# Two attention branches between dense products on one core: plain fp32 products grouped into eight bursts in two pairs of heads, score tiles at other distances, and the long branch's first turn taken from the first query tiles

## The chip, the cores and the metric

The kernel runs on one core of a Trainium2 chip. The metric is the device time of one execution in microseconds (us), lower is better. The program has 48,305 profiled instructions; nearly all of them are the work of one loop over eight blocks of 512 tokens.

## The reference

One encoder layer over 4096 tokens of width 1024, everything in fp32:

```python
h = rms_norm(x, norm_g)
proj = h @ w_in                      # 1024 -> 5376 columns, split into
(qa, ka, va, za, qb, kb, vb, zb, ga, gb)
# branch A: 8 query heads on 2 key heads of 64, own chunk of 64 and the one before,
#           partial rotary on qa and ka, an attention sink per head
# branch B: 8 heads of 64, own chunk and 8 chunks before, learned relative bias
ya = swa_sink_attention(rope(qa), rope(ka), va, sinks) * silu(za)
yb = chunked_relpos_attention(qb, kb, vb, rel_bias) * silu(zb)
merged = sigmoid(ga + bias0) * (ya @ w_br_a) + sigmoid(gb + bias1) * (yb @ w_br_b)
out = rms_norm(x + merged @ w_out, final_g)
```

## The kernel before, in words

**Blocks and pairs.** A block is 512 tokens, four tiles of 128. Its heads are worked off in eight pairs in the order 0, 4, 1, 5, 2, 6, 3, 7: pairs 0 to 3 are of branch A (the short branch, a query tile sees 256 keys), pairs 4 to 7 of branch B (the long branch, 640 keys). So short and long pairs alternate.

**Two kinds of product on TensorE.** The dense projections take three matmuls of 128x512 per slice of weights (high times high, low times high, high times low), on operands of type fp32r, lines L909 to L911. A "quarter" is six of them; a tile of weights has four quarters. Attention uses plain fp32 operands, in three steps:

- S0 to S3 ("scores"): the scores of query tile 0 to 3 of the *next* pair, L944 (short) and L953 (long), into the banks sc. VectorE then masks, adds the bias and takes the row maxima (L1242 to L1268); ScalarE takes the exponentials (E0 to E3, L1146) and so frees the score bank.
- T0, T1, ... ("turn_p"): a turn transposes up to four 128x128 pieces of the probabilities into the one bank ps_pt (L973). ScalarE (L1153) or VectorE (L1329) then copies the bank to one of four probs_t; a list per branch, A_OUT and B_OUT, says which (0 is ScalarE). PE waits before each turn until the turn before it is copied out.
- V0, V1, ... ("values"): probabilities times values into ps_o (L1004). Which keys a burst takes stands in A_BURSTS and B_BURSTS, which pieces a turn takes in A_TURNS and B_TURNS, as (half of the pair, key tile), where key tiles below 0 belong to the block before. The first V of a pair waits until VectorE has read the pair before out of ps_o (`whole`, L1366).

**The order.** All engines walk one list, PLAN, each taking from it its own steps; each engine works strictly in that order. Within a pair the order is written by hand in the strings A_BEATS and B_BEATS, where F is one quarter of dense products, T, V, S and E are the steps above, G and H the gating of the pair before, D the denominators. Each string has twelve F, so three tiles of weights. After the fourth F, and once a tile is at its second or third quarter, the step "norm" (N below) is put in: four transposes on PE into a bank of acc (L1013), read by VectorE (L1360).

**Rotary.** When a tile q or k of the short branch is complete, ScalarE copies it (pre, L1098) and rounds it (pre_hi, L1101), VectorE makes pre_lo (L1304) and pre*cos (L1308). PE multiplies by a permutation (L1024, L1025, called R below) into a bank of acc, and VectorE reads that (L1316), which frees the bank. For pairs 1, 2 and 3 the step R is put in front of a quarter of the following tile of weights, `fill[at_ + 3]` being that tile's fourth; for pair 0 and the keys it is in the list `lead`.

Of the kernel before, what the change touches and what calls it, by code (L numbers as in the profile page):

```python
# [24 lines left out]
D = 1024  # L25
# [22 lines left out]


A_TURNS = [[(0, 0), (1, 0)], [(0, 1), (1, 1)], [(0, 2), (1, 2)], [(0, 3), (1, 3), (0, -1), (1, -1)]]  # L50
B_TURNS = [[(0, -1)], [(1, -1)], [(0, 0)], [(1, 0)], [(0, -2)], [(1, -2)], [(0, 1)], [(1, 1)],
           [(0, -3), (1, -3)], [(0, 2), (1, 2)], [(0, -4), (1, -4), (0, 3), (1, 3)]]

A_BURSTS = [[0], [1], [2], [3, -1]]
B_BURSTS = [[-1], [0], [-2], [1], [-3], [2], [-4, 3]]

A_OUT = (0, 1, 1, 0)
B_OUT = (0, 1, 0, 1, 0, 0, 1, 0, 0, 1, 0)
RING = 4


def turns_of(s):
    return A_TURNS if s < PAIRS else B_TURNS


def bursts_of(s):
    return A_BURSTS if s < PAIRS else B_BURSTS

# [8 lines left out]
def segments(s, u, first):  # L77


    out, col = [], 0  # L80
    for hh, j in turns_of(s)[u]:
        if first and j < 0:
            continue
        t0, n = queries_of(s, j)
        out.append((hh, j, t0, n, col))
        col += n * P
    assert col <= BLK
    return out
# [27 lines left out]
O_BANKED = 2  # L116


A_BEATS = "T0 F G T1 V0 F H D T2 V1 S0 F E0 T3 V2 F S1 V3 F E1 F F S2 F E2 F F S3 F E3 F"
B_BEATS = "F T0 F G T1 F H D T2 V0 F T3 F T4 V1 S0 F T5 E0 F T6 V2 S1 F T7 E1 F T8 V3 S2 F T9 E2 V4 S3 T10 F E3 V5 F V6"  # L120
BEATS_QUARTERS = 12
NORM_AFTER = 4
EARLY = 1
# [6 lines left out]
def block_plan():  # L130
# [11 lines left out]
    def tile(name, n):  # L142
        i = TILES.index((name, n))
        return [[("mm", i, c)] for c in range(QUARTERS - 1)] + [[("mm", i, QUARTERS - 1), ("job", name, n)]]

    def tiles(first, last):

        return [g for t in TILES[TILES.index(first):TILES.index(last) + 1] for g in tile(*t)]

    q, v, k4 = tile("q", 0), tile("v", 0), tile("k", 4)  # L150
    lead = [[("mm", n, c)] for n in range(O_TILES) for c in range(QUARTERS)]
    lead[0] = [("claim_v",), *lead[0]]
    lead[-1] = [*lead[-1], ("v_out",)]
    lead += [*tile("k", 0), q[0], [*q[1], ("rope_in_k", 0)], q[2], [("rope_k", 0), *q[3]],
             v[0], [*v[1], ("rope_in", 0)], v[2], [("rope", 0), *v[3]], [("turn_v", 0), *k4[0]], *k4[1:], *tile("q", 4)]
    for t in range(TT):
        at_ = QUARTERS * O_TILES + 14 + t
        lead[at_] = [("scores", 0, t), *lead[at_], ("exps", 0, t)]
# [7 lines left out]
    fill = tiles(("z", 0), ("gb", AHEAD - 1))  # L166
    first_fill = TILES.index(("z", 0))
    for i in range(first_fill, TILES.index(("gb", AHEAD - 1)) + 1):
        name, s = TILES[i]
        at_ = QUARTERS * (i - first_fill + 1)  # L170
        if name == "q" and s < PAIRS:
            fill[at_] = [*fill[at_], ("rope_in", s)]
            fill[at_ + 3] = [("rope", s), *fill[at_ + 3]]
    fill += [[("mm", TILES.index(("br", 0)), 0)], [("mm", TILES.index(("br", 0)), 1), ("job", "ya", 0)]]

    for n, s in enumerate(ORDER):
        nxt = ORDER[n + 1] if n + 1 < SETS else None
        quarters = 0
        for beat in (A_BEATS if s < PAIRS else B_BEATS).split():
            kind, no = beat[0], int(beat[1:] or 0)  # L180
# [50 lines left out]
    for e in range(KT):  # L231
# [4 lines left out]
        for c in range(QUARTERS):  # L236
            plan.append(("mm", i, c))
            at_ = QUARTERS * e + c
# [21 lines left out]


PLAN = block_plan()


# [57 lines left out]
def turn_table(first):  # L322

    no, on = {}, [0, 0]
    for step in PLAN:
        if step[0] == "turn_p" and segments(step[1], step[2], first):
            engine = (A_OUT if step[1] < PAIRS else B_OUT)[step[2]]
            on[engine] += 1
# [1151 lines left out]
```

## Time and profile before

| what | value |
|---|---|
| median of 3 runs | 3419.65 us (3418.62 to 3423.51) |
| the profiled execution's own time | 3421.02 us |
| its span in the trace | 3419.2 us |
| TensorE matmuls busy | 3342.8 us, 98% |
| VectorE, ScalarE, GpSimd busy | 1482.7, 1422.4, 1309.1 us |
| granted TensorE clock | 0.999 |

The span begins with the first profiled instruction; the time of an execution lies 1.8 us above it. A busy TensorE is not one at its peak, because the ends of matmuls are modelled: what a stretch costs on PE is read from one start to the next.

### The profile page before, as it was taken

To read this page: it belongs to the slowest core of one execution; us is meant where nothing else is said; L and a number is where in the kernel's file an instruction comes from. 1 tells how busy PE (TensorE), PEld (TensorE's weight loads), DVE (VectorE), ACT (ScalarE), POOL (GpSimd) and SP (SyncE) were. 2 spreads that over 40 slices of the span, in tenths; PEclk is the share of its full clock that TensorE was granted. 3 is DMA by queue.
4 is the path that set the end of the run, shared out by engine and by line. 5 is a ranking of instruction groups with operands and counts; after the bars stand their busy time and mean duration, and the time that the engine had idled before them with its cause. 6 is when DMAs were issued, how large, how long until landed. Compare 5 with 4: busy or idle time off the path is not lost.

```text
span 3419.2 us, 48305 instructions
## 1 busy us (share of the span) xinstructions
PE 3342.8 (98%) x16328; PEld 2496.7 (73%) x16328; DVE 1482.7 (43%) x3097; ACT 1422.4 (42%) x2969; POOL 1309.1 (38%) x1087
## 2 busy tenths in 40 slices
PE   7999999999999999999999999999999999999998
PEld 6667876678766787667876678766787667876676
DVE  4662355513555135551355513555135551355512
ACT  4443444434444344443444434444344443444432
POOL 3334542344423454234542345423454234542244
PEclk9999999999999999999999999999999999999999
DMA  4212431124311242112421225211242112521123
GB/s 156 62 62 88 171 99 50 62 87 167 99 51 62 86 169 97 55 61 83 173 93 55 61 83 173 93 56 62 81 172 94 56 61 83 173 94 55 56 82 116
DMA packets 97782, 319.53 MB, mean 93 GB/s; under 512 B 9984, under 2 KB 26624, under 8 KB 95360
## 3 DMA queue, kind: packets, MB, share of 16 engines
q1 hardware_dynamic: 97536, 316.34, 28.5%
q8 instruction: 144, 2.36, 0.3%
q14 instruction: 102, 0.84, 0.1%
HBM read 299.52 MB, written 16.78 MB: 93 GB/s over the span
## 4 chain that ended last, share of the span: by engine, by line
PE 84%; issue 7%; DVE 5%; POOL 2%; ACT 1%; DMA 0%; DVEq 0%; POOLq 0%; SPq 0%; ACTq 0%
PE acc L909 16%; PE acc L911 14%; PE acc L910 14%; PE ps_o L1004 6%; PE ps_pt L973 5%; PE sc L953 3%; PE sc L909 3%; PE sc L911 3%; PE sc L910 3%; POOL w_lo L755 2%; PE sc L944 2%; PE sc L853 2%; PE sc L852 2%; PE sc L851 2%; PE sc L876 1%
## 5 line engine op out<-in xcount | busy, mean ns | idle before, releaser
L755 POOL TENSOR_TENSOR w_lo<-w_raw,w_hi 128x512 fp32r<-128x512 f32 x928 | 1210.3, 1310 | 2048.1 <-ACT w_hi L1058 2046.9
L909 PE MATMUL acc<-h_hi,w_hi 128*128 128x512 f32 x2432 | 1012.1, 416 | 15.5 <-DVE q L1316 15.5
L911 PE MATMUL acc<-h_hi,w_lo 128*128 128x512 f32 x2432 | 953.1, 392 | 0.0
L910 PE MATMUL acc<-h_lo,w_hi 128*128 128x512 f32 x2432 | 950.4, 391 | 0.0
L1058 ACT ACTIVATE w_hi<-w_raw 128x512 fp32r<-128x512 f32 x928 | 574.4, 625 | 393.1 <-DMA w_raw<-w 118.0
L909 PEld LDWEIGHTS acc<-h_hi,w_hi 128*128 128x128 f32 x2432 | 456.4, 188 | 228.5 <-issue 146.5
L911 PEld LDWEIGHTS acc<-h_hi,w_lo 128*128 128x128 f32 x2432 | 456.4, 188 | 101.7
L910 PEld LDWEIGHTS acc<-h_lo,w_hi 128*128 128x128 f32 x2432 | 458.1, 188 | 75.4
L1146 ACT ACTIVATE probs_b<-sc,negm 128x640 f32<-128x640 f32 x256 | 202.9, 794 | 390.3 <-DVE negm L1263 390.2
L1153 ACT ACTIVATE probs_t<-ps_pt 128x512 f32<-128x512 f32 (+1 forms) x272 | 150.7, 554 | 264.7 <-PE ps_pt L973 264.7
L1288 DVE SCALAR_TENSOR_TENSOR part<-th,sc 128x512 f32<-128x512 f32 x64 | 43.9, 686 | 467.9 <-PE sc L911 467.7
L1329 DVE COPY probs_t<-ps_pt 128x512 f32<-128x512 f32 (+1 forms) x188 | 125.3, 667 | 250.7 <-PE ps_pt L973 250.2
L1263 DVE TENSOR_REDUCE negm<-sc 128x1 f32<-128x640 f32 x256 | 211.0, 824 | 8.9
L909 PE MATMUL sc<-y_hi,w_hi 128*128 128x512 f32 x512 | 201.6, 394 | 6.0 <-DVE y_lo L1376 6.0
L911 PE MATMUL sc<-y_hi,w_lo 128*128 128x512 f32 x512 | 199.4, 390 | 0.0
L910 PE MATMUL sc<-y_lo,w_hi 128*128 128x512 f32 x512 | 199.3, 389 | 0.0
L973 PE MATMUL ps_pt<-ident,probs_b 128*128 128x128 f32 x1200 | 187.0, 274 | 6.2 <-DVE probs_t L1329 6.2
L973 PEld LDWEIGHTS ps_pt<-ident,probs_b 128*128 128x128 f32 x1200 | 147.6, 141 | 52.9 <-DVE probs_t L1329 8.6
L1255 DVE TENSOR_TENSOR sc<-sc,bias 128x256 f32<-128x256 f32 (+2 forms) x512 | 184.5, 360 | 2.9
L1116 ACT ACTIVATE th<-acc,gb_half 128x512 f32<-128x512 f32 x128 | 88.1, 688 | 218.9 <-PE acc L911 218.9
L1004 PE MATMUL ps_o<-probs_t,v_b 128*64 128x512 f32 (+1 forms) x960 | 175.9, 455 | 1.0 <-DVE probs_t L1329 0.3
L953 PE MATMUL sc<-k_b,q 64*128 64x320 f32 (+3 forms) x992 | 164.3, 448 | 3.6 <-ACT probs_b L1146 3.6
(140 smaller groups left out, 3916.4 us busy)
## 6 DMA issues: line engine op xcount, KB each, us to landing
w_raw<-w SPq DMA_DIRECT2D x464, 512.0 KB, 3.5
rows<-x SPq DMA_DIRECT2D x36, 512.0 KB, 7.4
xt<-x_t SPq DMA_DIRECT2D x16, 1024.0 KB, 10.0
out<-rows SPq DMA_DIRECT2D x32, 512.0 KB, 2.8
x_in<-x SPq DMA_DIRECT2D x28, 512.0 KB, 5.5
cs<-rope_tab SPq DMA_DIRECT2D x8, 512.0 KB, 4.3
bias<-near SPq DMA_DIRECT2D x1, 1024.0 KB, 13.5
g_out<-final_g SPq DMA_DIRECT2D x1, 512.0 KB, 11.6
```

What stands on the lines that cost most here:

```text
L755: pool.tensor_tensor(w_lo[n % 2][:, c], w_raw[n % 2][:, c], w_hi[n % 2][:, c].bitcast(FP32), ALU.subtract).then_inc(w_split, 1)
L909: pe.matmul(dst[:, :], hi, src_hi[:, k, :], start=begin, stop=False)
L910: pe.matmul(dst[:, :], hi, src_lo[:, k, :], start=False, stop=False)
L911: mm = pe.matmul(dst[:, :], lo, src_hi[:, k, :], start=False, stop=end)
L953: mm = pe.matmul(sc[hh][:, c, lo:B_HALF], q[n % 2][rows_, t * P:(t + 1) * P], k_b[rows_, s - PAIRS, t * P + c * B_HALF + lo:t * P + (c + 1 ...
L973: mm = pe.transpose(ps_pt[:, col + (t - t0) * P:col + (t - t0 + 1) * P], weights_of(s, hh, t)[:, r * P:(r + 1) * P], ident[:, :])
L1004: mm = pe.matmul(ps_o[HD * hh:HD * hh + HD, t0 * P:(t0 + n) * P], val, ring(first, turn)[:, col:col + n * P], start=j == every[0], stop=j ...
L1058: act.activation(w_hi[n % 2][:, c], w_raw[n % 2][:, c], ACT.Copy).then_inc(w_hi_done, 1)
L1146: act.activation(p_, score_tile(s, hh, t), ACT.Exp, bias=negm[:, POS[s] % 2, c:c + 1], accum_out=sums[:, POS[s] % 2, c:c + 1]).then_inc(pr ...
L1153: act.activation(ring(first, turn)[:, 0:n], ps_pt[:, 0:n], ACT.Copy).then_inc(pt_out[0], 1)
L1255: dve.tensor_tensor(dst, dst, tab, ALU.add).then_inc(scores_shaped, 1)
L1263: dve.tensor_reduce(nm, score_tile(s, hh, t), AX.XY, ALU.max, negate=True).then_inc(neg_ready, 1)
```

## The change

Five tables and two places in `block_plan` are edited. No instruction is added or removed; the order changes, and with it who copies out which turn.

```diff
-B_TURNS = [[(0, -1)], [(1, -1)], [(0, 0)], [(1, 0)], [(0, -2)], [(1, -2)], [(0, 1)], [(1, 1)],
-           [(0, -3), (1, -3)], [(0, 2), (1, 2)], [(0, -4), (1, -4), (0, 3), (1, 3)]]
+B_TURNS = [[(0, -3), (1, -3)], [(0, -1)], [(1, -1)], [(0, 0)], [(1, 0)], [(0, -2)], [(1, -2)], [(0, 1)],
+           [(1, 1)], [(0, 2), (1, 2)], [(0, -4), (1, -4), (0, 3), (1, 3)]]
-B_BURSTS = [[-1], [0], [-2], [1], [-3], [2], [-4, 3]]
+B_BURSTS = [[-1], [-3], [0], [-2], [1], [2], [-4, 3]]
-B_OUT = (0, 1, 0, 1, 0, 0, 1, 0, 0, 1, 0)
+B_OUT = (0, 1, 0, 1, 0, 1, 0, 0, 1, 1, 0)
-A_BEATS = "T0 F G T1 V0 F H D T2 V1 S0 F E0 T3 V2 F S1 V3 F E1 F F S2 F E2 F F S3 F E3 F"
-B_BEATS = "F T0 F G T1 F H D T2 V0 F T3 F T4 V1 S0 F T5 E0 F T6 V2 S1 F T7 E1 F T8 V3 S2 F T9 E2 V4 S3 T10 F E3 V5 F V6"
+A_BEATS = "T0 F G T1 F H D T2 V0 V1 S0 T3 F E0 F F S1 V2 V3 F E1 F F S2 F E2 F F S3 F E3"
+B_BEATS = "T0 F G T1 F H D T2 F T3 V0 V1 S0 F T4 E0 F T5 F T6 F V2 V3 S1 T7 F E1 T8 F T9 F V4 V5 S2 T10 F E2 F V6 S3 E3"
-    lead += [*tile("k", 0), q[0], [*q[1], ("rope_in_k", 0)], q[2], [("rope_k", 0), *q[3]],
-             v[0], [*v[1], ("rope_in", 0)], v[2], [("rope", 0), *v[3]], [("turn_v", 0), *k4[0]], *k4[1:], *tile("q", 4)]
+    lead += [*tile("k", 0), [*q[0], ("rope_in_k", 0)], q[1], [("rope_k", 0), *q[2]], q[3],
+             [*v[0], ("rope_in", 0)], v[1], [("rope", 0), *v[2]], v[3], [("turn_v", 0), *k4[0]], *k4[1:], *tile("q", 4)]
-            fill[at_ + 3] = [("rope", s), *fill[at_ + 3]]
+            fill[at_ + 2] = [("rope", s), *fill[at_ + 2]]
```

**Bursts.** Between two F of the beats there can stand a group with S or V in it. Before, a short pair has six such groups (T1 V0; T2 V1 S0; T3 V2; S1 V3; S2; S3) and a long pair seven (T2 V0; T4 V1 S0; T6 V2 S1; T8 V3 S2; T9 V4 S3 T10; V5; V6). Now each has four: T2 V0 V1 S0 T3, S1 V2 V3, S2 and S3 in a short pair, T3 V0 V1 S0, V2 V3 S1 T7, V4 V5 S2 T10 and V6 S3 in a long one. The last long pair of a block issues no S.

**From a long pair to a short one, ScalarE's row.** These are ScalarE's instructions in the loop over blocks, at the end of pair 5 and the start of pair 2, before the change. probs_a are the exponentials E3 of the short pair's last query tile, pre and pre_hi belong to the rotary of q3, and the last L1153 copies out the short pair's first turn T0.

```order
L1142 REGISTER_ALU
L1146 ACTIVATE probs_a_85,sums<-sc,negm 128x256
L581 ISA
L598 REGISTER_ALU
L1058 ACTIVATE w_hi_53<-w_raw_51 128x512
L542 REGISTER_ALU
L1097 REGISTER_ALU
L1098 ACTIVATE pre<-acc 128x512
L547 REGISTER_ALU
L1101 ACTIVATE pre_hi<-pre 128x512
L1152 REGISTER_ALU
L1153 ACTIVATE probs_t_76<-ps_pt 128x512
```

And now:

```order
L1098 ACTIVATE pre<-acc 128x512
L547 REGISTER_ALU
L1101 ACTIVATE pre_hi<-pre 128x512
L1142 REGISTER_ALU
L1146 ACTIVATE probs_a_84,sums<-sc,negm 128x256
L1142 REGISTER_ALU
L1146 ACTIVATE probs_a_85,sums<-sc,negm 128x256
L1152 REGISTER_ALU
L1153 ACTIVATE probs_t_76<-ps_pt 128x512
L1164 REGISTER_ALU
L1167 ACTIVATE y_hi<-whole 128x512
L1058 ACTIVATE w_hi_53<-w_raw_51 128x512
```

E3 stood ahead of a split of weights and the rotary copies; now it is the last thing in front of the copy of T0.

**From a short pair to a long one, PE's row.** This is PE between the last scores of pair 1 and the turn T1 or T0, before the change: the last of the three quarters behind S3, and then the long pair's first turn, of all four query tiles.

```order
L909 MATMUL acc<-h_hi,w_hi_53 128x512
L910 MATMUL acc<-h_lo,w_hi_53 128x512
L911 MATMUL acc<-h_hi,w_lo_55 128x512
L909 MATMUL acc<-h_hi,w_hi_53 128x512
L910 MATMUL acc<-h_lo,w_hi_53 128x512
L911 MATMUL acc<-h_hi,w_lo_55 128x512
L966 REGISTER_ALU
L973 MATMUL ps_pt<-ident,probs_b_72 128x128 x4
```

Now the first turn (two pieces of each half; its second row is the first one here) comes one quarter behind S3, and the turn of all four query tiles after one more:

```order
L973 MATMUL ps_pt<-ident,probs_b_73 128x128 x2
L801 REGISTER_ALU
L899 REGISTER_ALU
L909 MATMUL acc<-h_hi,w_hi_53 128x512
L910 MATMUL acc<-h_lo,w_hi_53 128x512
L911 MATMUL acc<-h_hi,w_lo_55 128x512
L909 MATMUL acc<-h_hi,w_hi_53 128x512
L910 MATMUL acc<-h_lo,w_hi_53 128x512
L911 MATMUL acc<-h_hi,w_lo_55 128x512
L966 REGISTER_ALU
L629 REGISTER_ALU
L973 MATMUL ps_pt<-ident,probs_b_72 128x128 x4
```

The turn of four query tiles moved one quarter nearer to the scores, and it stands behind another turn now.

**The rotary product of pair 2, PE's row,** within pair 1. Before, it follows the scores S2, and a quarter lies between the N step (L1013, in the row just above these) and it:

```order
L909 MATMUL acc<-h_hi,w_hi_53 128x512
L910 MATMUL acc<-h_lo,w_hi_53 128x512
L911 MATMUL acc<-h_hi,w_lo_55 128x512
L909 MATMUL acc<-h_hi,w_hi_53 128x512
L910 MATMUL acc<-h_lo,w_hi_53 128x512
L911 MATMUL acc<-h_hi,w_lo_55 128x512
L923 REGISTER_ALU
L953 MATMUL sc<-k_b,q_62 128x320 x4
L801 REGISTER_ALU
L1023 REGISTER_ALU
L1024 MATMUL acc<-pre_hi,perm_r 128x512
L1025 MATMUL acc<-pre_lo,perm_r 128x512
```

Now:

```order
L909 MATMUL acc<-h_hi,w_hi_53 128x512
L910 MATMUL acc<-h_lo,w_hi_53 128x512
L911 MATMUL acc<-h_hi,w_lo_55 128x512
L909 MATMUL acc<-h_hi,w_hi_53 128x512
L910 MATMUL acc<-h_lo,w_hi_53 128x512
L911 MATMUL acc<-h_hi,w_lo_55 128x512
L801 REGISTER_ALU
L1013 MATMUL acc<-ident,part 128x128 x4
L801 REGISTER_ALU
L1023 REGISTER_ALU
L1024 MATMUL acc<-pre_hi,perm_r 128x512
L1025 MATMUL acc<-pre_lo,perm_r 128x512
```

R follows N at once. Both write the same bank of acc, and by the kernel's rule of claims R waits until VectorE has read N out of it; that read (L1360) stands on VectorE behind the masks and maxima of S1, which PE issued one quarter earlier. VectorE's pre_lo and pre*cos (L1304, L1308), which stood behind those of S1, stand ahead of them now.

## Rows read from the trace of the kernel before

**Rows 1.** The page, part 1: busy time, share of the span, instructions.

```profile
PE 3342.8 (98%) x16328; PEld 2496.7 (73%) x16328; DVE 1482.7 (43%) x3097; ACT 1422.4 (42%) x2969; POOL 1309.1 (38%) x1087
```

**Rows 2.** The waits of PE: who for whom, us in total, times, longest.

```profile
PE acc L909 <- DVE q L1316: 15.5, 15, 1.7
...
PE ps_pt L973 <- DVE probs_t L1329: 6.2, 18, 1.1
```

**Rows 3.** Timeline of PE, a V alone between products: start us, us, instruction.

```profile
1015.75 0.40 PE L911 MATMUL acc<-h_hi,w_lo 128*128 128x512 f32 x1
1016.08 0.65 PE L1004 MATMUL ps_o<-probs_t,v_b 128*64 128x256 f32 x4
1016.66 0.50 PE L909 MATMUL acc<-h_hi,w_hi 128*128 128x512 f32 x1
1017.00 0.40 PE L910 MATMUL acc<-h_lo,w_hi 128*128 128x512 f32 x1
```

**Rows 4.** Timeline of PE, a turn alone between products.

```profile
1048.69 0.39 PE L911 MATMUL acc<-h_hi,w_lo 128*128 128x512 f32 x1
1048.92 0.60 PE L973 MATMUL ps_pt<-ident,probs_b 128*128 128x128 f32 x4
1049.27 0.48 PE L909 MATMUL acc<-h_hi,w_hi 128*128 128x512 f32 x1
1049.59 0.40 PE L910 MATMUL acc<-h_lo,w_hi 128*128 128x512 f32 x1
...
1050.75 0.60 PE L973 MATMUL ps_pt<-ident,probs_b 128*128 128x128 f32 x4
```

**Rows 5.** Timeline of all engines from S3 of short pair 2 on.

```profile
1013.58 0.59 PE L944 MATMUL sc<-k_a,q 64*128 64x192 f32 x4
...
1014.10 0.66 PE L973 MATMUL ps_pt<-ident,probs_b 128*128 128x128 f32 x4
1014.27 0.11 DVE L1242 MEMSET sc<- 128x64 f32 x1 [0.48 <-PE sc L944]
...
1014.52 0.47 PE L909 MATMUL acc<-h_hi,w_hi 128*128 128x512 f32 x1
...
1016.25 0.47 ACT L1146 ACTIVATE probs_a<-sc,negm 128x256 f32<-128x256 f32 x1 [0.40 <-DVE negm L1268]
...
1016.72 0.62 ACT L1058 ACTIVATE w_hi<-w_raw 128x512 fp32r<-128x512 f32 x1
```

**Rows 6.** Timeline of all engines from S3 of long pair 6 on.

```profile
1043.42 1.35 PE L953 MATMUL sc<-k_b,q 64*128 64x320 f32 x8
...
1044.70 0.50 PE L909 MATMUL acc<-h_hi,w_hi 128*128 128x512 f32 x1
...
1047.70 0.68 DVE L1366 TENSOR_TENSOR whole<-ps_o,gate 128x512 f32<-128x512 f32 x1
...
1047.82 0.80 ACT L1146 ACTIVATE probs_b<-sc,negm 128x640 f32<-128x640 f32 x1 [0.61 <-DVE negm L1263]
...
1048.61 0.62 ACT L1058 ACTIVATE w_hi<-w_raw 128x512 fp32r<-128x512 f32 x1
...
1049.61 0.59 ACT L1153 ACTIVATE probs_t<-ps_pt 128x512 f32<-128x512 f32 x1
```

**Rows 7.** Timeline of all engines, PE waiting for a turn's copy.

```profile
1057.05 0.68 DVE L1329 COPY probs_t<-ps_pt 128x512 f32<-128x512 f32 x1
...
1057.79 0.55 PE L973 MATMUL ps_pt<-ident,probs_b 128*128 128x128 f32 x3 [0.18 <-DVE probs_t L1329]
```

**Rows 8.** Timeline of all engines around pair 1's rotary product.

```profile
979.54 0.39 PE L911 MATMUL acc<-h_hi,w_lo 128*128 128x512 f32 x1
...
980.82 0.68 DVE L1316 TENSOR_TENSOR q<-acc,cs 128x512 f32<-128x512 f32 x1
...
981.63 0.49 PE L909 MATMUL acc<-h_hi,w_hi 128*128 128x512 f32 x1 [1.70 <-DVE q L1316]
```

**Rows 9.** Timeline of all engines from a rotary copy on.

```profile
1018.45 0.60 ACT L1098 ACTIVATE pre<-acc 128x512 f32<-128x512 f32 x1 [1.11 <-PE acc L911]
...
1019.74 0.69 DVE L1304 TENSOR_TENSOR pre_lo<-pre,pre_hi 128x512 fp32r<-128x512 f32 x1 [3.52 <-ACT pre_hi L1101]
...
1021.14 0.68 DVE L1366 TENSOR_TENSOR whole<-ps_o,gate 128x512 f32<-128x512 f32 x1
...
1022.08 0.65 PE L1004 MATMUL ps_o<-probs_t,v_a 128*64 128x256 f32 x4 [0.75 <-DVE whole L1366]
```

## The prediction, as it was put on record

> **What bounds the kernel now.** I read the page first: matmuls are busy for 98% of the span while the other three engines stand below 45% [rows 1]. So PE sets the end, and only two things can move the time: what PE's own row costs from start to start, and how long PE stands still. The table of waits shows that it hardly stands still: its two largest groups inside the loop are 15.5 us for VectorE's read of a rotary product and 6.2 us for turns that are not copied out yet [rows 2]. Then I read the timeline for the price of changing between the two kinds of product. The reader is to look at starts, since ends are modelled. Products start 0.23 us apart, and a turn comes 0.23 us behind a product too (1048.69 to 1048.92) [rows 4]. But a V comes 0.33 us behind one (1015.75 to 1016.08), and behind the V the second product starts 0.34 us after the first (1016.66 to 1017.00) [rows 3]. So a group that holds S or V costs 0.10 going in and 0.11 coming out, 0.21 in all. A turn alone costs 0.35 itself (1048.92 to 1049.27) and some 0.09 on the way out [rows 4]. A quarter behind it takes 1.48 (1049.27 to 1050.75); without a neighbour of the other kind it is six times 0.23, about 1.37. What is left to ask is what the new order makes PE wait for.
>
> **The change part by part, in a block of the loop.**
>
> *Fewer bursts.* A short and a long pair have 6 + 7 groups with S or V now and 4 + 4 after: five fewer at 0.21 is 1.05 us. The last two pairs of a block lose four only, since there no S separates the tail: 0.84. The sum is 3 x 1.05 + 0.84 = 4.0 us gained. Turns that lose or find a neighbour among V and S I take as even: a turn behind S costs 0.42 (1014.10 to 1014.52) [rows 5] instead of 0.35, and saves the group's exit in exchange.
>
> A page of the Trainium skill speaks against that gain. "TensorE: Matmul & The Clock Gate", Part 2, says that PE pulls the next weight load ahead of matmuls in flight, so that a stream's spacing is its columns. By that a border between kinds of product would cost nothing and joining bursts would give 0 instead of 4.0. Rows 3 show 0.10 and 0.11 of it on either side of a V, and I go by the rows.
>
> *From a long pair to a short one (three times in a block).* The new order is V6 S3 E3, T0, one quarter, T1. PE may issue T1 only when ScalarE has copied T0 out, and ScalarE, which works in order, has E3 in front of that copy. From the start of S3, ScalarE is free behind E3 at 1016.72 - 1013.58 = 3.14 us [rows 5]. The copy takes 0.59 [rows 6], and PE starts a matmul 0.06 behind a copy's end (1057.05 + 0.68 to 1057.79) [rows 7]: T1 cannot start before 3.79. PE arrives there after S3 0.52, T0 0.42 and a quarter 1.48 = 2.42. The wait is 1.37. Before, T10, three quarters and V5, V6 stood between S3 and T1. Queued behind T1 on PE is everything else; behind E3 on ScalarE stand the copy, y_hi and a split, which nobody needs that early.
>
> *From a short pair to a long one (four times).* The order is S3, quarter, E3, T0, quarter, T1. From S3's start ScalarE is free at 1048.61 - 1043.42 = 5.19 [rows 6]; with copy and release 5.84. PE arrives after 1.28 + 1.48 + 0.35 + 1.48 = 4.59. The wait is 1.25. T0 itself needs only query tiles 0 and 1 and goes through at once; but that doesn't help, because its copy stands behind E3. The turn of all four tiles needed E3 before as well, and came three quarters behind S3, just after it: 1048.92 against an exponential that ends by 1048.7 [rows 6]. Together: 3 x 1.37 + 4 x 1.25 = 9.1 us of new waits per block, and no work that hides them.
>
> *The rotary steps.* Pair 1 waits 2.09 - 0.23 = 1.86 now (979.54 to 981.63), because the bank is read by VectorE only behind S2's masks and maxima [rows 8]; pair 0 a few tenths, some 2.4 together. After, that wait goes, but R stands directly behind N, and both need the same bank. In pair 1, from S0's end: ScalarE is behind E0 at 3.91 (1048.61 - 1044.70) [rows 6], splits for some 0.5, starts pre at 4.4; VectorE is through with pre_lo and the cosine 2.69 later (1018.45 to 1021.14) [rows 9], at 7.1; S1's masks and maxima take 3.0 (1044.70 to 1047.70) [rows 6], N's read 0.68: 10.8. PE arrives at R at 9.0 (T3 0.42, three quarters 4.3, S1 1.28, V2 and V3 1.16, quarter 1.48, N 0.35). The wait is 1.8. In pair 0 the new R needs pre_lo, which is behind S2's 3.0: 3.0 + 0.69 + 0.06 against two quarters, 2.85: 0.9. In pair 2 R's read is behind S0: 0.1. Sum 2.8 for 2.4, so +0.4. In the lead both R come a quarter earlier, and pre_lo is ready some 2.0 after its tile, against 2.74 for two quarters: nothing changes.
>
> *What goes away.* V0 of pair 2 waits 0.75 for `whole` [rows 9]; V0 now stands two quarters later: -0.75. Of the 6.2 us for turns' copies in eight blocks [rows 2], perhaps two thirds: -0.5. *What comes:* in the last pair V6 stands directly behind T10 and waits for its copy, and twice a z tile's read stands before T8's copy: +0.5 together. The even distances of the score tiles give nothing else: PE's waits for score banks are too small to stand among the rows.
>
> The queues: SP's row is the same, so all loads keep their order; keep_k on GpSimd stands one quarter later, on an engine that idles for more than half the time [rows 1].
>
> **The sum.** Per loop block: 9.1 + 0.4 + 0.5 - 1.25 - 4.0 = +4.75. Seven such blocks make 33. In the first block the turns of key tiles below 0 don't exist, so a long pair's first turn comes late and the four waits of 1.25 fall away: 3 x 1.37 - 4 x 4 x 0.21 = +0.7. Together +34. Made on the profiled execution's own 3421.0 that is 3455; that execution lies 1.4 above the median of the runs, 3419.65, so on the scale of the runs **3453**, 1.0% slower.
>
> **Rivals.**
>
> *Covered waits: faster.* If ScalarE got to T0's copy before PE needs T1, the 9.1 fell away and -4.35 x 7 - 3.4 = -34 were left: 3386. This would need that the copy doesn't stand behind E3, or that a wait elsewhere on the way (of V0, N or R) already holds PE up so that it arrives late. For it speaks that ScalarE is busy only 42% [rows 1]; against it that its row is fixed and E3's start hangs on VectorE's maxima, which come one after the other. It decides from 0.62 us per crossing on: seven crossings at that price are what the rest gives (4.35). I find 1.25 and 1.37, twice that. Chance 0.08.
>
> *Half of each: no change.* If the crossings cost half (shorter chains behind S3 than in rows 5 and 6, which were taken where ScalarE had nothing else), +34 became about +2: 3421. Chance 0.05.
>
> *Joining bursts gives nothing.* Should the price of a border only move to another place, as when the weight load of the next product is late behind any attention matmul, then V to S would cost what V to product costs: 3453 + 7 x 4.0 + 3.4 = 3484. Against it: a turn that follows S costs 0.42 [rows 5], less than the 0.35 + 0.09 of one alone, so a neighbour of the same kind does spare the border. By the Trainium skill's rule on early weight loads this would be the result too, for the other reason. Chance 0.04.
>
> *More waits than I see.* A VectorE that is late by the rotary's 1.4 us at S1, or a slow cosine, could push E1 and with it S2: up to +1 per block, 3461. That lies inside the forecast.
>
> **How the numbers follow.** The forecast, slower by 20 to 48 us, has 0.80: its lower end takes the crossings at 1.0 instead of 1.3 (-15), its upper the burst gain at half (+14). The range that leaves out two in ten is 3436 to 3470. Slower by over 0.2% (7 us, about what a measurement of this kernel can tell from no change): 0.80 + 0.04 + 0.02 from worse cases = 0.86. Within 0.2%: 0.05. Faster: 0.09.
>
> **What the profile of the changed kernel would show.** Right: in each crossing T1 starts 5.8 (short to long) and 3.8 us (long to short) behind the start of S3, in the table of waits PE ps_pt L973 goes from 6 to over 55 us and ScalarE's copy L1153 is the releaser; R in pair 1 waits for VectorE's read of N; 8 groups with S or V per two pairs; V0 has no wait for `whole`. Wrong: T1 comes 1.48 behind T0 without a gap; or the copy of T0 starts before E3; or a V behind a V costs as much as one behind a product.

## The result, and the profile after

| what | before | after |
|---|---|---|
| median of 4 runs each | 3419.39 us (3418.62 to 3423.51) | 3457.94 us (3455.12 to 3463.2) |
| the profiled execution's own time | 3421.02 us | 3455.18 us |
| its span in the trace | 3419.2 us | 3453.4 us |
| granted TensorE clock | 0.999 | 0.995 |

The changed kernel is slower by about 1.1%: the ratio is 1.0108, with a 95% interval of 1.0092 to 1.0125. The forecast was 3453, within 3436 to 3470.

Page of the kernel after, busy time of each engine, to be read beside [rows 1]:

```profile
PE 3307.2 (96%) x16328; PEld 2504.8 (73%) x16328; DVE 1547.3 (45%) x3125; ACT 1412.6 (41%) x2941; POOL 1306.5 (38%) x1087
```

PE is busy 36 us less over a span 34 us longer. So the products did become cheaper, and something else took more than that back. The table of PE's waits (waited for, then total us, times, longest us) says what, beside [rows 2]:

```profile
PE ps_pt L973 <- ACT probs_t L1153: 60.8, 52, 1.7
PE acc L1024 <- DVE gate L1360: 22.5, 8, 4.0
PE ps_pt L823 <- DVE spread L1186: 12.8, 1, 12.8
PE ps_pt L973 <- DVE probs_t L1329: 8.4, 25, 1.0
PE sc L909 <- DVE y_lo L1376: 6.0, 8, 0.8
PE acc L1024 <- DVE pre_lo L1304: 6.0, 8, 0.8
...
PE ps_o L1004 <- ACT probs_t L1153: 5.3, 8, 0.7
```

The first row did not exist before: 52 waits for a turn's copy on ScalarE. The third is the program's first wait, the same in both kernels (12.9 us before). The second and the sixth are the rotary product R, behind the read of N and behind pre_lo; the row of before that they replace, L909 behind q, 15.5 us [rows 2], is gone.

Both crossings look as they were worked out. Short to long, timeline of PE, then of ScalarE:

```profile
937.44 0.40 PE L911 MATMUL acc<-h_hi,w_lo 128*128 128x512 f32 x1
938.89 0.66 PE L973 MATMUL ps_pt<-ident,probs_b 128*128 128x128 f32 x4 [1.05 <-ACT probs_t L1153]
```

```profile
937.46 0.80 ACT L1146 ACTIVATE probs_b<-sc,negm 128x640 f32<-128x640 f32 x1
938.15 0.19 ACT L1146 ACTIVATION_READ_ACCUMULATOR probs_b<-sc,negm 128x1 f32 x1
938.25 0.59 ACT L1153 ACTIVATE probs_t<-ps_pt 128x512 f32<-128x512 f32 x1
```

T0 had been issued a quarter earlier, but its copy starts at 938.25, the moment the second exponential of E3 is over, and T1 starts 0.05 behind its end. The last product before T1 started at 937.44, 1.45 us ahead of it where 0.23 would do, so PE lost 1.22 us (the idle time of 1.05 in the row is counted from the product's modelled end). Long to short:

```profile
1030.29 0.40 PE L911 MATMUL acc<-h_hi,w_lo 128*128 128x512 f32 x1
1031.89 0.66 PE L973 MATMUL ps_pt<-ident,probs_a 128*128 128x128 f32 x4 [1.21 <-ACT probs_t L1153]
```

Here PE lost 1.60 - 0.23 = 1.37 us; the other two crossings of this kind in the block cost 1.38 and 1.53, and all four from short to long cost 1.22.

The rotary step is where the size was wrong. Pair 1 of a later block, PE, VectorE and GpSimd:

```profile
1843.41 0.60 PE L1013 MATMUL acc<-ident,part 128*128 128x128 f32 x4
1846.65 0.50 PE L1024 MATMUL acc<-pre_hi,perm_r 128*128 128x512 f32 x1 [2.64 <-DVE gate L1360]
...
1847.68 0.40 PE L911 MATMUL acc<-h_hi,w_lo 128*128 128x512 f32 x1
1847.91 0.39 PE L909 MATMUL acc<-h_hi,w_hi 128*128 128x512 f32 x1
...
1849.38 0.63 PE L910 MATMUL acc<-h_lo,w_hi 128*128 128x512 f32 x1
1849.80 0.63 PE L911 MATMUL acc<-h_hi,w_lo 128*128 128x512 f32 x1
```

```profile
1840.53 0.72 DVE L1304 TENSOR_TENSOR pre_lo<-pre,pre_hi 128x512 fp32r<-128x512 f32 x1 [2.62 <-ACT pre_hi L1101]
1841.35 1.57 DVE L1308 TENSOR_TENSOR pre<-pre,cs 128x512 f32<-128x512 f32 x1
1843.01 0.11 DVE L1252 MEMSET sc<- 64x64 f32 x1
...
1845.10 0.82 DVE L1263 TENSOR_REDUCE negm<-sc 128x1 f32<-128x640 f32 x1
1845.84 0.68 DVE L1360 TENSOR_TENSOR gate<-acc,z 128x512 f32<-128x512 f32 x1
```

```profile
1841.09 1.28 POOL L755 TENSOR_TENSOR w_lo<-w_raw,w_hi 128x512 fp32r<-128x512 f32 x1 [0.40 <-ACT w_hi L1058]
```

R starts 3.24 us behind the start of N (1843.41 to 1846.65), where 0.35 would do: a wait of 2.89. (The row's 2.64 counts from the modelled end of N; the expectations below, which speak of 2.55, took 0.35 off the 2.91 behind the last of N's four transposes.) In front of the read of N stand S1's masks and maxima (1843.01 to 1845.8), and they are late because pre*cos took 1.57 us instead of the 0.69 that a multiplication of this size takes elsewhere. It began while GpSimd worked on w_lo. That this is the cause is borne out by the whole trace: the 24 cosines that began during a w_lo took 1.57 to 1.62 us, the other 16 took 0.69. The kernel before has 16 of the slow kind too, two in each block, for the steps in `lead`, where no wait of PE for them stands in its table; in the pairs it has none. And 1.5 us behind the wait the products start 0.43 apart (1849.38 to 1849.80) instead of 0.23: for some seven products the granted clock is 0.50, the lower of its two levels (1.2 instead of 2.4 GHz). Such a stretch stands behind this wait in six of the eight blocks; before, there was none inside the loop.

### The profile page after: what moved, and what is told of

It is laid out like the page before. It is cut to its first block, busy times and chain, and to the rows that moved or that the text cites. A ratio compares the mean times of both kernels' runs of the same rounds, so it can differ in the third digit from the quotient of the medians.

```text
span 3453.4 us, 48311 instructions
## 1 busy us (share of the span) xinstructions
PE 3307.2 (96%) x16328; PEld 2504.8 (73%) x16328; DVE 1547.3 (45%) x3125; ACT 1412.6 (41%) x2941; POOL 1306.5 (38%) x1087
## 4 chain that ended last, share of the span: by engine, by line
PE 82%; DVE 7%; issue 7%; ACT 3%; POOL 0%; DMA 0%; DVEq 0%; ACTq 0%; SPq 0%; POOLq 0%
PE acc L909 14%; PE acc L911 13%; PE acc L910 13%; PE ps_pt L973 5%; PE ps_o L1004 5%; PE sc L909 3%; PE sc L911 3%; PE sc L910 3%; PE sc L953 3%; PE sc L851 2%; PE sc L853 2%; PE sc L852 2%; PE sc L944 1%; DVE sc L1255 1%; DVE negm L1263 1%
## 5 line engine op out<-in xcount | busy, mean ns | idle before, releaser
L909 PE MATMUL acc<-h_hi,w_hi 128*128 128x512 f32 x2432 | 1006.8, 414 | 0.1
L909 PEld LDWEIGHTS acc<-h_hi,w_hi 128*128 128x128 f32 x2432 | 459.0, 189 | 128.0 <-issue 49.4
L1153 ACT ACTIVATE probs_t<-ps_pt 128x512 f32<-128x512 f32 (+2 forms) x244 | 137.0, 561 | 475.2 <-PE ps_pt L973 475.2
L1329 DVE COPY probs_t<-ps_pt 128x512 f32<-128x512 f32 (+1 forms) x216 | 140.8, 652 | 258.2 <-PE ps_pt L973 258.2
L973 PE MATMUL ps_pt<-ident,probs_b 128*128 128x128 f32 x1200 | 190.5, 277 | 34.3 <-ACT probs_t L1153 29.8
L973 PEld LDWEIGHTS ps_pt<-ident,probs_b 128*128 128x128 f32 x1200 | 141.9, 141 | 97.9 <-ACT probs_t L1153 35.7
L909 PE MATMUL sc<-y_hi,w_hi 128*128 128x512 f32 x512 | 201.4, 393 | 6.0 <-DVE y_lo L1376 6.0
L1004 PE MATMUL ps_o<-probs_t,v_b 128*64 128x512 f32 (+1 forms) x960 | 156.6, 446 | 5.3 <-ACT probs_t L1153 5.3
```

The source lines that it names most:

```text
L909: pe.matmul(dst[:, :], hi, src_hi[:, k, :], start=begin, stop=False)
L973: mm = pe.transpose(ps_pt[:, col + (t - t0) * P:col + (t - t0 + 1) * P], weights_of(s, hh, t)[:, r * P:(r + 1) * P], ident[:, :])
L1004: mm = pe.matmul(ps_o[HD * hh:HD * hh + HD, t0 * P:(t0 + n) * P], val, ring(first, turn)[:, col:col + n * P], start=j == every[0], stop=j ...
L1329: dve.tensor_copy(ring(first, turn)[:, 0:n], ps_pt[:, 0:n]).then_inc(pt_out[1], 1)
```

## The experiments

Every ratio is to the kernel before, run on the same chip in the same session.

**1. The copy of T0 ahead of E3, for short pairs.** The changed kernel with a new step X: E3 of a short pair stands behind T0 and its copy.

```diff
-A_BEATS = "T0 F G T1 ..."
+A_BEATS = "T0 X F G T1 ..."
-B_BEATS = "... V6 S3 E3"
+B_BEATS = "... V6 S3"
```

> The changed kernel, but E3 of a short pair is put behind the copy of its first turn T0 on ScalarE. Crossing theory (T1 waits because T0's copy stands behind E3): the waits of about 1.4 us behind T0 at the three crossings from a long to a short pair vanish, 3 x 1.4 x 8 = 33 us less than the changed kernel, about 3422 to 3427; the four other crossings keep 1.22. Rival (the slow-down is the rotary wait behind N and the stretches of half clock that follow it): under 8 us gained, since T1 would only wait for the exponentials instead.

Measured: 3434.15 (3433.53 to 3437.05), ratio 1.0043 (1.0026 to 1.0060). 24 us came back, not 33. The waits:

```profile
PE ps_pt L977 <- ACT probs_t L1157: 29.9, 28, 1.1
PE ps_pt L977 <- DVE probs_t L1333: 22.9, 47, 1.3
```

ScalarE's half is gone; VectorE's copies now hold PE, 22.9 us where it was 8.4: PE arrives sooner at turns of the short pairs whose copies stand behind pre*cos and `whole`, or behind the denominators. The mechanism stands, the gain was passed on in part.

**2. The first copy on VectorE, for long pairs.**

```diff
-B_OUT = (0, 1, 0, 1, 0, 1, 0, 0, 1, 1, 0)
+B_OUT = (1, 1, 0, 1, 0, 1, 0, 0, 1, 1, 0)
```

> The changed kernel, but the long branch's first turn is copied out by VectorE (first entry of B_OUT is 1), which is free behind S3's maxima while ScalarE still does E3. Crossing theory: T1 then waits for E3 itself (5.19 from S3's start plus some 0.1) and not for a copy behind it, so 1.22 falls to about 0.7 at three of the four crossings from short to long (at pair 0 a z tile stands ahead on VectorE): 3 x 0.5 x 7 = 10 us gained, about 3447. Rival (T1 was held by E3 alone): no change.

Measured: 3450.24 (3448.88 to 3452.55), ratio 1.0087 (1.0070 to 1.0103), 8 us back where 10 were expected. T1 now waits for E3 itself, up to 0.6 us ("ACT probs_b", 13.2 us in 21 waits).

**3. The rotary product back where it was** in the loop, all else as changed.

```diff
-fill[at_ + 2] = [("rope", s), *fill[at_ + 2]]
+fill[at_ + 3] = [("rope", s), *fill[at_ + 3]]
```

> The changed kernel with the rotary product of pairs 1 to 3 back in front of the fourth quarter of the following tile (fill[at_ + 3]); the lead as changed. Theory: R in pair 1 comes one quarter after N, so its wait of 2.55 falls to about 1.2; R in pair 0 (0.9) no longer waits, and VectorE's late read of it is hidden in the wait at the crossing; the stretches at half clock behind R vanish, since PE stands still for a shorter time. 8 x (1.35 + 0.9) + 10 for the clock = 28 us, about 3430, and the runs lie closer together. Rival (clock stretches come from the crossings' waits or are chance): only 18 us and half clock stays.

Measured: 3432.21 (3430.84 to 3435.6), ratio 1.0036 (1.0024 to 1.0049). This one step is worth 26 us of the changed kernel, 3.2 a block, and no stretch of lower clock is left in the loop.

**4. The kernel before, with the bursts of the short pairs joined**, and nothing else.

```diff
-A_BEATS = "T0 F G T1 V0 F H D T2 V1 S0 F E0 T3 V2 F S1 V3 F E1 F F S2 F E2 F F S3 F E3 F"
+A_BEATS = "T0 F G T1 F H D T2 V0 V1 S0 F E0 T3 F F S1 V2 V3 F E1 F S2 F E2 F F S3 F E3 F"
```

> The kernel before, with bursts joined in the short pairs alone (T2 V0 V1 S0; S1 V2 V3 one quarter later), long pairs, crossings and rotary as before. Theory: per short pair two groups fewer at 0.21 and two joints of V and V at 0.15 each (the V behind a V took 0.43 in the changed kernel instead of 0.58), so 4 x 0.72, plus 0.75 for V0 in pair 2, minus a new wait of up to 1.4 for S2 in pair 1, where VectorE does pre_lo and pre*cos ahead of S1: 2.2 us per block, 3402. If a border costs nothing (the rule on early weight loads): 0.75 less and 1.4 more per block, 3424.

Measured: 3417.55 (3416.74 to 3419.93), ratio 0.9991 (0.9982 to 1.0001): a miss. S2 of pair 1 now comes sooner than its score bank is free:

```profile
977.27 0.40 PE L911 MATMUL acc<-h_hi,w_lo 128*128 128x512 f32 x1
979.68 1.03 PE L953 MATMUL sc<-k_b,q 64*128 64x320 f32 x4 [2.01 <-ACT probs_b L1146]
```

This costs some 2.1 us a block, with the same pre*cos at 1.59 us ahead of the masks, and the lower clock stands behind it in seven of the eight blocks. Since waits of before went at the same time (V0 for `whole`, 5.2 us, and 6.2 us of the row for q), the table of waits grew by 4.4 us only, from 49.1 to 53.5 without the program's first wait. The larger part of the joins' gain went to the clock: its mean is 0.995 instead of 0.999, which is up to 14 us of this span.

**5. Scores of the short pairs a quarter earlier**, with the last quarter between E3 and T0.

```diff
-A_BEATS = "... F E1 F F S2 F E2 F F S3 F E3"
+A_BEATS = "... F E1 F S2 F E2 F F S3 F E3 F"
```

> The changed kernel, with the score tiles S2 and S3 of a short pair one quarter (64 products of a projection) earlier, so that the last quarter stands between E3 and the long branch's T0. If the wait of T0 after a short pair is only for the exponentials of S3 on ScalarE (the trace shows 1.22 us in front of T0 at each of four crossings of a block, and four quarters of cover would be about 14.6 us of products), it goes: 4 x 1.22 x 7 to 8 blocks = 34 to 39 us, less some for the new place of the rotation of pair 1 behind S3: 3424 us (3418 to 3432). If the wait is a price of the change from one kind of product to another and not of ScalarE, nothing changes: 3458 us. The waits of the long pairs (1.38 to 1.53 us, three per block) stay by either theory.

Measured: 3439.07 (3437.7 to 3441.68), ratio 1.0052 (1.0036 to 1.0067), 19 us of the expected 34. (The expectation has two slips: the wait stands in front of T1, not T0, and a quarter is six matmuls, not 64.) R within pair 0 lost its wait, and T1 behind pair 0 waits 0.26 only, but at the other three crossings to a long pair T1 still waits 0.86 to 0.95 (start to start 1.09 to 1.18). The quarter that moved also completes a tile, and with it two more ScalarE steps, a rounded weight tile and the projection's own copy, come to stand ahead of T0's copy. The wait is for the queue, whatever is in it.

**6. Values apart.** The changed kernel with S between the two V of each group; groups and their borders stay.

```diff
-"... T2 V0 V1 S0 T3 ..." / "... V0 V1 S0 ... V2 V3 S1 ... V4 V5 S2 ..."
+"... T2 V0 S0 V1 T3 ..." / "... V0 S0 V1 ... V2 S1 V3 ... V4 S2 V5 ..."
```

> The changed kernel, with the score tile between the two turns of values of its group (V0 S0 V1 instead of V0 V1 S0) in all groups that have two turns and a score tile. Groups and their borders to the projections stay as they were; only which plain products stand behind which changes. Theory from the trace of the changed kernel: a turn of values behind a turn of values costs 0.15 us less than behind a score tile or a projection, 2 such places of a short pair and 3 of a long one are given up: 2 x 4 + 3 x 4 less the one in the last pair = about 19 places a block x 0.15 = 2.9 us a block, 8 blocks: +23 us, 3480 us (3472 to 3486). Rival, the prediction's own count, by which only the number of groups counts: 3458 us, within 3 us. A second rival: the score tile that stands earlier is earlier at ScalarE and takes 0.3 to 0.6 us from waits behind it: 3450 us.

Measured: 3474.01 (3473.07 to 3478.08), ratio 1.0154 (1.0139 to 1.0170), 16 us above the changed kernel; between the two profiled executions it is 23. Two V together, in the changed kernel:

```profile
1342.11 1.08 PE L1004 MATMUL ps_o<-probs_t,v_a 128*64 128x256 f32 x8
1343.12 0.54 PE L953 MATMUL sc<-k_b,q 64*128 64x320 f32 x2
```

and the same two apart:

```profile
1355.19 0.65 PE L1004 MATMUL ps_o<-probs_t,v_a 128*64 128x256 f32 x4
1355.77 1.35 PE L953 MATMUL sc<-k_b,q 64*128 64x320 f32 x8
1357.05 0.65 PE L1004 MATMUL ps_o<-probs_t,v_a 128*64 128x256 f32 x4
1357.63 0.55 PE L973 MATMUL ps_pt<-ident,probs_a 128*128 128x128 f32 x3
```

1.01 together, 0.58 + 0.58 apart: 0.15 for each V behind a V. By single starts, the four steps within the two joined V take 0.27, 0.22, 0.22 and 0.32 us: the first is longer by 0.05 and the last by 0.10, and two V apart pay both twice. Seventeen such places of a block make 2.6 us, about 20 over eight blocks. The rival by which only the number of groups counts is out.

**7. The rotary product alone.** The kernel before, with nothing but this.

```diff
-fill[at_ + 3] = [("rope", s), *fill[at_ + 3]]
+fill[at_ + 2] = [("rope", s), *fill[at_ + 2]]
```

> The kernel before, with nothing but the rotation's product one quarter earlier in the pairs of the loop (two quarters behind the read-in instead of three). Theory from the trace of the changed kernel: behind the denominators' product in pair 1 the rotation waits 2.5 us, 0.9 us in pair 0, and the clock falls to half for 3.4 us behind the long wait, together 2.8 to 3.3 us a block less what waits there before (1.4 us): +12 to +25 us, 3432 to 3446 us, with spells of half clock in most blocks. Rival, the prediction's term (+0.4 us a block): 3423 us, within 3 us, no half clock.

Measured: 3416.79 (3415.79 to 3418.9), ratio 0.9990 (0.9980 to 0.9999). My expectation was wrong by 15 us or more: the same edit that cost 26 us in the changed kernel costs nothing here. Pair 1:

```profile
1401.49 0.60 PE L1013 MATMUL acc<-ident,part 128*128 128x128 f32 x4
1403.26 0.49 PE L1024 MATMUL acc<-pre_hi,perm_r 128*128 128x512 f32 x1 [1.17 <-DVE gate L1360]
```

```profile
1400.31 0.82 DVE L1263 TENSOR_REDUCE negm<-sc 128x1 f32<-128x640 f32 x1
1401.06 0.68 DVE L1304 TENSOR_TENSOR pre_lo<-pre,pre_hi 128x512 fp32r<-128x512 f32 x1
1401.84 0.69 DVE L1308 TENSOR_TENSOR pre<-pre,cs 128x512 f32<-128x512 f32 x1
1402.45 0.68 DVE L1360 TENSOR_TENSOR gate<-acc,z 128x512 f32<-128x512 f32 x1
```

In the old order S1's masks are done before pre_lo, so the read of N follows the cosine at once, and the cosine, with GpSimd not yet at w_lo, takes 0.69. The wait is 1.17 instead of 2.64, and no clock is lost behind it. So the 26 us belong neither to the joined bursts nor to the rotary edit, but to the two together: the joined order put S1's masks between the cosine and the read of N, and the cosine beside w_lo.

**8. All waits out, in steps.** Five kernels look for the order in which the joins are kept and the waits are not. The first takes the step X of experiment 1, the scores of experiment 5, A_OUT (0, 1, 0, 0), B_OUT with its ninth entry at 0, and each R a quarter or so further from what it waits for.

```diff
-A_BEATS = "T0 F G T1 F H D ... F E1 F F S2 F E2 F F S3 F E3"
+A_BEATS = "T0 X F T1 G F H D ... F E1 F S2 F E2 F F S3 F E3 F"
-fill[at_] = [*fill[at_], ("rope_in", s)]
-fill[at_ + 2] = [("rope", s), *fill[at_ + 2]]
+first, at_rope = {1: (0, 1), 2: (2, 2), 3: (1, 2)}[s]
...
```

> A try for the fastest order: the changed kernel's groups, with the first turn's copies ahead of E3 on ScalarE and on VectorE for the fourth, the scores of the short pairs a quarter earlier with a quarter behind E3, and the rotation a quarter or two further from what it waits for in all three pairs. If each wait that the traces showed (1.22 and 1.38 to 1.53 at crossings, 2.55 and 0.89 at rotations, the spells of half clock behind the longest) is gone and the joins bring what they measured (0.21 for each group joined, 0.15 more for values behind values, about 6.8 us a block), the block takes 426.5 - 6.8 - 2.2 = 417.5 us: 3350 to 3365 us, ratio about 0.982. If waits move on to VectorE as they did when the copy alone was moved (T1 and T3 of the short pairs, 1.1 and 0.8 us) it ends at 3385 to 3400 us. If joining gave nothing (groups cost the same however they stand), 3410 to 3425 us.

Measured: 3397.46 (3395.77 to 3399.93), ratio 0.9932 (0.9918 to 0.9946): faster than both kernels, but not by what I hoped. T1 of the long pairs still waits, as in experiment 5. The second kernel has `B_OUT[0] = 1` and takes in the tile of the rotary step within pair 2 one place earlier.

> The previous best order (3397.5 us) with two numbers changed: the copy of T0 of a long pair goes to VectorE (B_OUT[0] = 1), and the rotation of pair 2 is read in one step earlier. Theory: the trace of the previous one shows T1 of a long pair 0.8 to 0.95 us late at three crossings of a block, because the copy of T0 stands on ScalarE behind a rounded weight tile and the projection's k_b or q tile, while VectorE is idle for 2.5 us there; and 1.39 us of TensorE's wait for VectorE's q in pair 2, behind y_lo and two score tiles. Both go: 3 x 0.85 + 1.39 = 3.9 us a block, x 8 = 31: 3366 us (3360 to 3376). Rival: the copies add to VectorE's queue in front of the denominators and the masks, and the wait moves on as it did when the copy alone was moved: 3385 to 3397 us.

Measured: 3393.38 (3390.08 to 3394.52), ratio 0.9921 (0.9908 to 0.9935). Against 3366 expected this is a miss. T1 waits no longer at three of the four crossings to a long pair; the fourth, behind pair 0, was worse:

```profile
1347.16 0.40 PE L916 MATMUL acc<-h_hi,w_lo 128*128 128x512 f32 x1
1349.91 0.66 PE L978 MATMUL ps_pt<-ident,probs_b 128*128 128x128 f32 x4 [2.35 <-DVE probs_t L1334]
```

Behind pair 0 the finished tile is a z. VectorE's step for it waits for ScalarE's th, which stands behind E3, and T0's copy stands behind that step. The copy had changed its queue and met the same E3. The third kernel puts E3 behind that copy for the long pairs too (B_BEATS begins "T0 X F G T1") and the copy on ScalarE again.

> The previous order, with the exponentials E3 of the scores for a long pair put behind the copy of that long pair's T0 (as was done for the short pairs), and that copy on ScalarE again (B_OUT[0] = 0). Theory: a crossing waits for what stands ahead of T0's copy in its engine's queue, whichever engine it is. The previous kernel's trace has 2.3 us of TensorE's wait at the crossing from pair 0, where VectorE waits for ScalarE's th, which stands behind E3 and a rounded weight tile, and the clock at half behind it. With E3 out of the way th and the copy come about 1.6 us earlier: 2.3 plus 1 for the clock less what is left, 2.3 to 3 us a block, x 8: 3372 us (3366 to 3382). Rival: E3 behind the copy is late for T1's or T2's copy and for the first products of the pair, and gives as much away: 3390 us.

Measured: 3397.3 (3397.2 to 3398.25), ratio 0.9929 (0.9916 to 0.9943): no better, where 3372 was expected. With E3 behind the copy, the exponentials themselves come late for T1, 27.8 us in all:

```profile
PE ps_pt L978 <- ACT probs_b L1151: 27.8, 28, 1.1
```

The fourth kernel is this one with the copy on VectorE:

> As the run before, with the copy of T0 of a long pair on VectorE (B_OUT[0] = 1). If ScalarE's queue (a rounded weight tile and the projection's tile, 1.2 us) still holds the copy with E3 gone, this one is faster by 0.3 to 0.8 us at each of three crossings, 7 to 19 us: 3360 us; at the crossing from pair 0 VectorE waits for th with or without it. If E3 was all that was in the way, the two are within 4 us.

Measured: 3384.35 (3383.24 to 3386.32), ratio 0.9889 (0.9874 to 0.9905), a gain of 13 us, inside the 7 to 19 expected though above the 3360 named. The same row is at 14.2 us. The fifth keeps E3 behind the copy for the first long pair alone:

> The last order with one choice made crossing by crossing: E3 behind the copy of T0 only at the crossing from pair 0 (where VectorE would wait for ScalarE's th), and ahead of it, as in the one before the last two, at the other three. Theory: the waits at these three, 0.65 to 0.75 us each (T1 waits for the exponentials E3 themselves), go, as they had gone two runs ago, and that of pair 0 stays at 0.65 us instead of 2.3: 3 x 0.7 x 7 to 8 blocks = 15 to 17 us off 3384: 3369 us (3364 to 3374). If a freed wait comes back elsewhere in the pair, 3380 to 3385 us.

```diff
-elif kind == "X" and n:
+elif kind == "X" and n and (s < PAIRS or n == 1):
```

with the matching condition on E. Measured: **3368.69 (3368.37 to 3370.57), ratio 0.9852 (0.9835 to 0.9868)**. It came out where it was expected, has the changed kernel's eight groups, and is 1.5% faster than the kernel before and, by the two ratios, 2.5% faster than the changed one. Its waits, and the largest that is left in the loop:

```profile
PE ps_pt L828 <- DVE spread L1191: 12.7, 1, 12.7
PE ps_pt L978 <- ACT probs_t L1158: 8.4, 27, 0.6
PE sc L914 <- DVE y_lo L1381: 6.1, 8, 0.8
PE acc L914 <- DVE q L1321: 5.8, 8, 1.4
```

## Why the prediction was right, and where it was not

**The sign and the crossings: right.** 1.22 against 1.25, and 1.37 to 1.53 against 1.37; 9.2 a block against 9.1. L973 behind ScalarE's L1153 stands at 60.8 us, "over 55". V0's wait for `whole` is gone. Experiments 1, 2 and 5 show that what counts is the queue ahead of the copy. The rival of covered waits named what it would need, that the copy doesn't stand behind E3; the last kernel does that at the three crossings to a short pair and at one to a long pair, has the copy on VectorE at all four of the latter, and came out 52 us faster than before, further on that side than the rival's 3386.

**The joins: right in direction, the term mis-sized.** Predicted 4.0 a block, 31 us in all. The last kernel measures it nearly free of the rest: its span is 3419.2 - 3366.6 = 52.6 us below that of before, the rows of its table of waits (without the first wait of the program) sum to 46.0 against 49.1, and the clock is the same 0.999. That leaves 49.5 us, 6.2 a block. What was missing is the 0.15 for a V behind a V, which I had not looked for; I had priced only the borders to the projections. Twenty such places in a full block make 3.0, so the two prices together come out some 0.8 above what was measured; where that went is not shown. My sign of being wrong, "a V behind a V costs as much as one behind a product", did not appear: it costs less, and by more than the border. By the Trainium skill's page "TensorE: Matmul & The Clock Gate", Part 2, joining should have given nothing; 49.5 us decide against it for this mix of fp32r and plain fp32 products.

**The rotary steps: mis-sized.** I gave the wait behind N 1.8, and counted the same way it was 2.89; pair 0's was 0.89 against 0.9. Of the missing 1.1, 0.9 is the cosine, for which I took a duration of 0.7 from [rows 9]; at its new place GpSimd is at work beside it and it takes 1.57. "Or a slow cosine" stood among the waits that I might not see, priced at up to 1 a block. The trace of before could have said more: 16 of its 40 cosines are slow, each of them begun during a w_lo.

**The clock: not foreseen.** Seven products at 0.43 instead of 0.23 are 1.4 us; six such stretches make some 8 us. I leave out the program's first 40 us, where several runs have a stretch as well. Behind them, the kernels that waited for 2 us or more in most blocks (after, experiments 1, 2, 4, 5 and 6, and the second of 8) have such stretches, though not behind each of those waits, and one behind a wait of 1.94 us (experiment 6). Those of experiments 3, 7 and 8 (the other four) and the kernel before have none. Their waits stay at 1.7 or less, but for one in the first block of experiment 3 (2.6) and one in that of the first kernel of 8 (2.3). That the waits bring the stretches rests on this comparison; what decides in the single case is not shown.

**Small ones.** T9 behind a z tile waits 0.42 and 0.50, and V6 waits 0.7 for T10's copy: some 1.6 a block, where the prediction had put 0.5 for the three together. VectorE's copies cost 8.4 us and not the third of 6.2 that I left of them.

**Why the sum fits.** It fits better than its terms, and that is in part luck. Joins gave 18 us more than predicted; the rotary wait took some 9, the clock some 8, and the waits for turns' copies (VectorE's 8.4 and V6's 5.3, where some 6 had been put) some 8. The crossings, the largest term, were exact, and they set the sign. Between the profiled executions the kernel lost 34 us, as forecast; by these terms it would be some 7 more, which stay unassigned, since waits read from start to start and those of the table differ by up to 0.25 each. Between the medians it lost 39.

## What to carry to other kernels

When work on the engine that sets the time is brought together, look at each answer that it waits for and price what is queued ahead of it on the engine that gives it. The busy share doesn't tell: at 41% busy, ScalarE cost this kernel 60 us. Moving the step to an idle engine helps only if nothing in front of it there waits for the first one. The gain of joining and the loss at the crossings were separable, so it was worth keeping the edit and mending the order, crossing by crossing.

## What the runs showed of the hardware

- Two V, plain fp32 matmuls of 128x256, take 1.01 us side by side and 1.16 apart, with scores or a turn between them. Between fp32r products and plain fp32 ones a border costs 0.10 in and 0.11 out [rows 3].
- A VectorE product of two SBUF tiles of 128x512 took 0.69 us alone and 1.57 when it began while GpSimd's w_lo (1.28 us) ran: it ended at 1842.92, 0.55 behind w_lo's end at 1842.37. In all 14 traces of this case every cosine begun during a w_lo took 1.57 to 1.62 us and every other 0.69 or 0.70. The Trainium skill's page "SBUF — State Buffer", in "SBUF: two separate sides", says that a VectorE operation with two SBUF inputs and a GpSimd one that reads SBUF lock each other out; this trace agrees: from the cosine's start to w_lo's end are 1.02 us, and the cosine lost 0.88.
- Behind waits of 1.9 to 4.0 us in the loop the granted clock was at its lower level (0.50, 1.2 GHz) for seven products or so in most blocks, so that such a wait cost some 1.4 us more than its length. No wait of 1.7 us or less in the loop had such a stretch behind it.
